# Attention core: the scores of a query tile move from two tiles ahead to three, with a third buffer of probabilities

## What is computed

```python
mask = key_chunk[None, :] <= q_chunk[:, None]
s = jnp.einsum('bqhd,bkhd->bhqk', q_blk, k).astype(jnp.float32) * scale
s = jnp.where(mask[None, None], s, neg)
prob = jax.nn.softmax(s, axis=-1).astype(v.dtype)
return jnp.einsum('bhqk,bkhe->bqhe', prob, v)
```

## Time and profile before

| | |
|---|---|
| median of 3 runs | 1248.72 us |
| profiled execution: its own time | 1248.54 us |
| its span, first to last instruction | 1246.7 us |
| granted TensorE clock, mean | 0.998 |
| TensorE busy (records of matmuls) | 1233.4 us, 99% |
| VectorE, ScalarE, GpSimd busy | 719.9, 483.8, 514.3 us |
| the four attention heads | from 281.6 to 391.1 us of the span |

### The profile page before, as it was taken

The page is one execution under the profiler, slowest core; times in us unless marked ns, Lnnn a source line. Parts: engine busy times, 40 slices in busy tenths (PEclk is TensorE's granted clock), DMA queues, the critical chain, the costliest instruction groups (busy, mean ns, idle before and its releaser), DMA issues.

```text
span 1246.7 us, 16762 instructions
## 1 busy us (share of the span) xinstructions
PE 1233.4 (99%) x6006; PEld 1040.8 (83%) x6006; DVE 719.9 (58%) x1172; ACT 483.8 (39%) x892; POOL 514.3 (41%) x515
## 2 busy tenths in 40 slices
PE   9999999999999999999999999999999999999997
PEld 8888888888898888888888888888888888888886
DVE  5544444466664437845444445444499999954433
ACT  7622222256664225533333333333354344424422
POOL 2533343351110003555533455433499889810011
PEclk9999999999999999999999999999999999999999
DMA  9511101000021500243332342422555545420002
GB/s 343 165 35 49 36 2 43 1 18 18 17 104 50 152 1 1 76 127 101 111 121 71 105 127 85 127 90 80 186 199 157 169 169 189 149 85 1 1 34 101
DMA packets 101931, 115.09 MB, mean 92 GB/s; under 512 B 4832, under 2 KB 67680, under 8 KB 101856
## 3 DMA queue, kind: packets, MB, share of 16 engines
q1 hardware_dynamic: 101424, 113.57, 28.0%
q10 hardware_dynamic: 432, 0.54, 0.1%
HBM read 90.49 MB, written 23.59 MB: 92 GB/s over the span
## 4 chain that ended last, share of the span: by engine, by line
PE 96%; DVE 2%; ACT 1%; issue 1%; DMA 0%; POOLq 0%; DVEq 0%; SPq 0%; POOL 0%; ACTq 0%
PE PS L1749 11%; PE PS L1750 11%; PE PS L1748 11%; PE PS L206 8%; PE PS L208 8%; PE PS L207 8%; PE PS L2082 5%; PE PS L2084 5%; PE PS L2083 5%; PE PS L1043 3%; PE PS L1059 3%; PE PS L2461 2%; PE PS L2460 2%; PE PS L2459 2%; PE PS L871 2%; PE PS L2474 2%
## 5 line engine op out<-in xcount | busy, mean ns | idle before, releaser
L206 PE MATMUL PS<-WF,HTH 128*128 128x512 f32 (+1 forms) x448 | 176.5, 394 | 0.2 <-DVE HTL L436 0.2
L208 PE MATMUL PS<-WF,HTL 128*128 128x512 f32 (+1 forms) x448 | 173.3, 387 | 0.0
L207 PE MATMUL PS<-WF,HTH 128*128 128x512 f32 (+1 forms) x448 | 172.9, 386 | 0.0
L1469 DVE TENSOR_TENSOR X<-X,PS 128x512 f32<-128x512 f32 x172 | 110.2, 678 | 54.4 <-PE PS L208 37.3
L1748 PE MATMUL PS<-HTH,WF 128*128 128x512 f32 x336 | 130.7, 389 | 0.0
L1749 PE MATMUL PS<-HTL,WF 128*128 128x512 f32 x336 | 130.7, 389 | 0.0
L1750 PE MATMUL PS<-HTH,WF 128*128 128x512 f32 x336 | 130.7, 389 | 0.0
L1681 DVE TENSOR_TENSOR WF<-RAW,WF 128x512 fp32r<-128x512 f32 x63 | 70.9, 1126 | 77.5 <-ACT WF L1671 77.5
L1748 PE MATMUL PS<-WF 128*128 128x512 f32 x252 | 98.0, 389 | 0.0
L1749 PE MATMUL PS<-WF 128*128 128x512 f32 x252 | 98.0, 389 | 0.0
L1750 PE MATMUL PS<-WF 128*128 128x512 f32 x252 | 98.0, 389 | 0.0
(11 more groups left out here) (266 smaller groups left out, 2808.0 us busy)
## 6 DMA issues: line engine op xcount, KB each, us to landing
hid<-TMP SPq DMA_DIRECT2D x74, 256.0 KB, 2.3
TMP<-hid SPq DMA_DIRECT2D x25, 512.0 KB, 4.4
RAW<-in_w_ffn_gate SPq DMA_DIRECT2D x22, 512.0 KB, 4.2
RAW<-in_w_ffn_up SPq DMA_DIRECT2D x22, 512.0 KB, 5.4
RAW<-in_w_ffn_down SPq DMA_DIRECT2D x22, 512.0 KB, 4.2
X<-in_x SPq DMA_DIRECT2D x16, 512.0 KB, 5.7
RAW<-in_w_in SPq DMA_DIRECT2D x32, 256.0 KB, 3.6
TAB<-hid SPq DMA_DIRECT2D x9, 512.0 KB, 4.6
```

The lines of the kernel that those rows point to most:

```text
L206: nc.tensor.matmul(dst, HTH[:, k, tok], w_h, start=(k == 0), stop=False)
L207: nc.tensor.matmul(dst, HTH[:, k, tok], w_l, start=False, stop=False)
L208: last = nc.tensor.matmul(dst, HTL[:, k, tok], w_h, start=False, stop=(k == K - 1))
L1469: nc.vector.tensor_tensor(x, x, src, ALU.add).then_inc(done, 1)
```

## The change

- TensorE: the filler is now `scores(t + 3)` in slots 0 to 4, and `early(0)`, `early(1)`, `early(2)` in slots 5, 6 and 7. Slot 1 is no longer without one.
- The next head's first queries (rows 0 to 511) are made in two halves of three matmuls (`first_queries`), one in slot 5 and one in slot 6; the second six matmuls (rows 512 to 1023) stay in slot 7. In head 3 the fillers of slots 5, 6 and 7 are two, one and one retention tiles.
- ScalarE: the exponentials go two tiles ahead: `exp(t + 2)` in slot t. The split of the next head's weights moves from slot 3 to slot 2, on VectorE too. The output weights' copies stay in slots 4 and 5.
- VectorE: slot t holds `divide(t + 1)`, `biggest(t + 3)`, `out_lo(t - 1)`.
- A third buffer of probabilities (JUNK, in TAB), and three columns each for biases and sums.
- The banks of scores are handed out in another order, and `scores(4)` waits for two exponentials instead of three.

The diff, cut to its core:

```diff
--- before.py
+++ after.py
@@ -977,6 +977,15 @@
             three(bank(2 + b), [([WQ[x][:, k] for x in range(2)], [CT[y][:, k, blk] for y in range(2)])
                                 for k in range(2)]).then_inc(a_proj, 1)
 
+        def first_queries(e, h, k):
+
+            if k == 0:
+                e.wait_ge(a_w_lo, h * 2 + 2)
+            for n, (x, y) in enumerate(((0, 0), (0, 1), (1, 0))):
+                last = nc.tensor.matmul(bank(2), WQ[x][:, k], CT[y][:, k, 0:HALF], start=(k + n == 0), stop=(k * n == 2))
+            if k == 1:
+                last.then_inc(a_proj, 1)
+
         def head_keys(e, h, blocks=(0, 1)):
 
             for b in blocks:
@@ -1017,7 +1026,12 @@
 
             return (1, (t + 1) * P) if t < 4 else (2, (t + 1) * P // 2)
 
-        SCORE_BANK = (2, 0, 3, 1, 2, 0, 2, 0)
+        SCORE_BANK = (2, 3, 0, 1, 2, 0, 2, 0)
+        BIAS, SUMS = 85, 88
+
+        def probs(t):
+
+            return JUNK if t % 3 == 2 else tmp((t % 3) * 1024, 1024)
 
         def score_banks(t):
 
@@ -1031,7 +1045,7 @@
                 if t in (0, 2):
                     e.wait_ge(a_qr, h * 2 + (2 if t else 1))
                 if t >= 4:
-                    e.wait_ge(a_exp, h * T + t - 1)
+                    e.wait_ge(a_exp, h * T + (2 if t == 4 else t - 1))
                 tok = slice(t * P, t * P + P)
                 nb, n = seen(t)
                 for c in range(nb):
@@ -1048,7 +1062,7 @@
                 e.wait_ge(a_pt, h * T + t)
                 for j in range(t + 1):
                     last = nc.tensor.transpose(PS[:, 4 + j // 4, (j % 4) * P:(j % 4) * P + P],
-                                               tmp((t % 2) * 1024 + j * P, P), ident)
+                                               probs(t)[:, j * P:j * P + P], ident)
                 last.then_inc(a_turn, 1)
 
             def values(t):
@@ -1062,14 +1076,11 @@
             for t in range(3):
                 scores(t)
             for t in range(T):
-                if t == 0:
-                    scores(3)
-                elif 2 <= t < T - 2:
-                    scores(t + 2)
-                elif t >= T - 2:
-
-                    e.wait_ge(a_exp, h * T + T - 1)
-                    early(t + 2 - T)
+                if t < T - 3:
+                    scores(t + 3)
+                else:
+                    e.wait_ge(a_exp, h * T + (T if t == T - 1 else T - 1))
+                    early(t + 3 - T)
                 if t >= 1:
                     values(t - 1)
                 turn(t)
@@ -1088,11 +1099,11 @@
         def act_head(e, h, early, late, after, turned=None):
             def exp(t):
                 e.wait_ge(a_bias, h * T + t + 1)
-                e.wait_ge(a_turn, h * T + max(0, t - 1))
+                e.wait_ge(a_turn, h * T + max(0, t - 2))
                 nb, n = seen(t)
-                dst = tmp((t % 2) * 1024, nb * n).rearrange("p (b n) -> p b n", b=nb)
-                nc.scalar.activation(dst, score_banks(t), ACT.Exp, bias=ST[:, 76 + t % 2:77 + t % 2],
-                                     scale=SCALE, accum_out=ST[:, 78 + t % 2:79 + t % 2]).then_inc(a_exp, 1)
+                dst = probs(t)[:, 0:nb * n].rearrange("p (b n) -> p b n", b=nb)
+                nc.scalar.activation(dst, score_banks(t), ACT.Exp, bias=ST[:, BIAS + t % 3:BIAS + 1 + t % 3],
+                                     scale=SCALE, accum_out=ST[:, SUMS + t % 3:SUMS + 1 + t % 3]).then_inc(a_exp, 1)
 
             def out_hi(t):
                 e.wait_ge(a_pv, h * T + t + 1)
@@ -1100,16 +1111,17 @@
                                bank(6 + t % 2, P).unsqueeze(1)).then_inc(a_o_hi, 1)
 
             exp(0)
+            exp(1)
             for t in range(T):
-                if t + 1 < T:
-                    exp(t + 1)
+                if t + 2 < T:
+                    exp(t + 2)
                 if turned and t == T - 1:
                     turned(1)
                 if t >= 1:
                     out_hi(t - 1)
                 if turned and t == T - 2:
                     turned(0)
-                if t == 3:
+                if t == 2:
                     early()
                 if t in (4, 5):
                     out_weights_hi(e, h, t - 4)
@@ -1126,7 +1138,7 @@
         def dve_head(e, h, early, after, turned=None):
             def biggest(t):
                 e.wait_ge(a_scores, h * T + t + 1)
-                e.wait_ge(a_exp, h * T + max(0, t - 1))
+                e.wait_ge(a_exp, h * T + max(0, t - 2))
                 src = score_banks(t)
                 nb, n = seen(t)
 
@@ -1135,7 +1147,7 @@
                 nc.vector.tensor_reduce(ST[:, 74 + t % 2:75 + t % 2], src, mybir.AxisListType.XY if nb > 1 else AXX,
                                         ALU.max).then_inc(a_max, 1)
                 e.wait_ge(a_max, h * T + t + 1)
-                nc.vector.tensor_scalar(ST[:, 76 + t % 2:77 + t % 2], ST[:, 74 + t % 2:75 + t % 2], -SCALE, None,
+                nc.vector.tensor_scalar(ST[:, BIAS + t % 3:BIAS + 1 + t % 3], ST[:, 74 + t % 2:75 + t % 2], -SCALE, None,
                                         ALU.mult).then_inc(a_bias, 1)
 
             def out_lo(t):
@@ -1147,26 +1159,27 @@
             def divide(t):
                 e.wait_ge(a_exp, h * T + t + 1)
                 n = (t + 1) * P
-                nc.vector.reciprocal(ST[:, 80 + t % 2:81 + t % 2], ST[:, 78 + t % 2:79 + t % 2]).then_inc(a_rec, 1)
+                nc.vector.reciprocal(ST[:, 80 + t % 2:81 + t % 2], ST[:, SUMS + t % 3:SUMS + 1 + t % 3]).then_inc(a_rec, 1)
                 e.wait_ge(a_rec, h * T + t + 1)
-                p = tmp((t % 2) * 1024, n)
+                p = probs(t)[:, 0:n]
                 nc.vector.tensor_scalar(p, p, ST[:, 80 + t % 2:81 + t % 2], None, ALU.mult).then_inc(a_prob, 1)
 
             biggest(0)
             biggest(1)
             divide(0)
+            biggest(2)
             for t in range(T):
-                if t + 2 < T:
-                    biggest(t + 2)
                 if t + 1 < T:
                     divide(t + 1)
+                if t + 3 < T:
+                    biggest(t + 3)
                 if turned and t == T - 1:
                     turned(1)
                 if t >= 1:
                     out_lo(t - 1)
                 if turned and t == T - 2:
                     turned(0)
-                if t == 3:
+                if t == 2:
                     early()
             after()
             out_lo(T - 1)
@@ -1178,17 +1191,23 @@
             e.wait_ge(b_qr, 5)
             head_keys(e, 0, [1])
 
+            def next_queries(b, h):
+                if b < 2:
+                    first_queries(e, h, b)
+                else:
+                    head_queries(e, h, 1)
+
             def next_keys(values, h):
                 head_keys(e, h)
                 values()
             with e.Fori(0, HEADS - 1) as h:
-                pe_head(e, h, lambda b: head_queries(e, h + 1, b), lambda values: next_keys(values, h + 1))
+                pe_head(e, h, lambda b: next_queries(b, h + 1), lambda values: next_keys(values, h + 1))
             e.wait_ge(r_done, NR)
 
             def first_turns(b):
                 if b:
                     e.wait_ge(a_exp, NR)
-                pe_retention_turn(e, (2 * b, 2 * b + 1))
+                pe_retention_turn(e, (b + 1,) if b else (0, 1))
 
             def out_products(values):
                 out_product(e, 0)
```

## The result

The changed kernel takes 1254.26 us (median of 6 runs, 1254.06 to 1254.96) where the kernel before takes 1249.01 (6 runs, 1248.57 to 1249.36): ratio 1.0045, 95% interval 1.0034 to 1.0055. It is slower by 5.2 us; forecast was 1253.5, range 1250.9 to 1255.4. The profiled execution took 1254.27 us with a span of 1252.4, against 1248.54 and 1246.7.

The account below looks back on a forecast made before the run. TensorE, busy 1233.4 of 1246.7 us, was taken as the bound. Heads 0 to 2 added 3.7 us and head 3 1.3, so 5.0 on 1248.54: 1253.5 us, range 1250.9 to 1255.4.

Parts of the forecast that it names:

- Slots 0 to 2: Front of heads 0 to 2: slot 1's gaps go, 1.02 us idle comes ahead of tile 5's scores; net +0.07 us each.
- Both old gaps: TensorE, slot 1: 0.64 us idle ahead of tile 0's values, 0.41 us ahead of tile 1's transposes; both would go.
- Slot 5, slot 6: Shorter fillers leave TensorE waiting for ScalarE's copy: 0.58 us idle ahead of tile 4's values, 0.55 us ahead of tile 5's.
- Heads 0 to 2: Each of the first three heads slower by 0.07 + 0.58 + 0.55 + 0.03 = 1.23 us, 3.7 in all.
- Head 3: Last head, retention transposes as fillers: 0.06 + 0.37 + 0.74 + 0.1 = 1.3 us slower.
- The rivals: Whole kernel: bubbles go, 1244.8 us (0.04); move is even, 1248.8 us (0.08); ScalarE gets behind, 1255.5 us and up (0.08).
- No buffer of probabilities was short: Slot 1's gaps: a skill rule blamed too few buffers, 3.7 us gain; the prediction said no buffer's release ends them.
- ScalarE did not fall behind: Third rival, slots 4 and 5: long exponentials of tiles 6 and 7 delay result and copy, 1255.5 us and up; chance 0.08.
- the second rival: The move is even: slots 1 and 2 only shift the gap, copies keep pace in slots 5 and 6; 1248.8 us, chance 0.08.
- the way without the weights: Slots 5 and 6, ScalarE's chain behind the values without the output weights' copy (0.52 us): 1.27 to 1.35 us.
- The unknowns that the prediction lists: Score start after a wait, -0.4 to +1.2 us over four heads; slots 5 and 6 waits, 0.2 each, 1.6 in all.
- its 3.7 us of idle time: TensorE's idle in slot 1 before the change: some 1.0 us each in heads 0, 1 and 2, 0.7 in head 3.

Follow-up runs that it names:

- The swap on VectorE: Changed kernel with the maximum of tile 3 ahead of the division of tile 1 on VectorE, nothing else: 1252.28 us.
- tile 7 split: Changed kernel with tile 7's scores cut in two over slots 4 and 5, its exponential in slot 6, queries whole in slots 6 and 7: 1250.06 us.
- split of tile 4 and two moves: Kernel before, changed banks, tile 4's scores halved over slots 1 and 2, output weights behind the copy, slot 7's copy between the query splits: 1245.38 us.

## Why the prediction was right

- *Slots 0 to 2.* Both old gaps went and one of 0.92 us came (1.02 forecast), at the place and with the releaser named; the hand-over was 0.06 and not 0.09, and values and transposes ahead of it ended 0.06 later in the head than laid out. Forecast +0.07; measured, from first score to first score of tile 6, 320.79 - 311.73 = 9.06 against 9.01 for the same work before (318.99 - 309.98): +0.05. The swap on VectorE shows the cause. The prediction said rightly that no buffer's release ends the old gaps. It named banks 0 and 1 for the new one, but did not draw from it that this gap is a wait for a buffer.
- *Slot 5, slot 6.* 0.58 and 0.55 forecast, 0.59 and 0.55 measured. Putting long fillers back (tile 7 split) takes them away.
- *Heads 0 to 2.* 1.23 forecast each, 1.36 measured. The term that was missing: behind a wait the values take longer, ten from 328.99 to 330.18 in 1.19 us where they took 1.12, twelve in 1.41 from 332.05 (to the transposes at 333.46) where they took 1.34. That is 0.07 us for each of the two new waits; why is not shown.
- *Head 3.* 1.3 forecast, 1.32 measured, and by the parts that were named. The scores of tile 6 start 379.93 - 371.26 = 8.67 us into the head, against 8.61 for the same work before: +0.06. The values of tile 4 start 388.00 - 386.32 = 1.68 us behind the end of those of tile 3 (1.67 forecast). From the end of the values of tile 4 to those of tile 5 it is 1.78 us, with four retention transposes between where there were eight and 1.79: as forecast, taking them out shortened nothing.
- *The rivals.* No buffer of probabilities was short (third buffer alone: 109.50 us against 109.49). Of the banks for the scores this is not shown: the kernel uses all eight, and no run gave tile 5 a bank that was free. ScalarE did not fall behind: in head 1 the exponential of tile 7 ended at 330.00, and ScalarE then waited 0.47 us for the values of tile 4. One sentence of the second rival was wrong: I put the way without the weights at 1.27 to 1.35 us. With them behind the copy, from the end of the values of tile 3 to the start of those of tile 4 it is 328.20 - 326.66 = 1.54 us, and 331.14 - 329.39 = 1.75 one tile later, since the copy waits for the transposes (0.19 us in its row). The same slip made the one large miss among the expectations.
- *The total.* 5.0 forecast, 5.40 in the heads, 5.25 between the medians of the two kernels.
- *What was off beside it.* The unknowns that the prediction lists add up to -2.0 and +2.8 us, which is 1251.5 to 1256.3; the range of 1250.9 to 1255.4 is not their sum. And its 3.7 us of idle time leave out a wait in heads 0 to 2 of the kernel before, 0.29 us ahead of the last values (334.86 to 336.62, less 1.47). It is in the changed kernel as well and moves no term of the forecast.

## What to carry to other kernels

A filler has to be counted over the whole loop: moving scores one slot ahead filled the empty slot at the front and took a filler from the end, where the wait for the copy had been hidden by it. Look at the length of what is moved: cutting a piece at its bank and spreading it over two slots gave 2.5 us, where moving it whole gave 0.5 us in the heads and nothing clear of the noise between the medians. And before giving a tile another buffer or an earlier place, ask whether its wait ends with a result or with the release of a buffer, of which buffer, and by what chain: here the old gaps ended with a copy and a division, the new one with a bank, and VectorE's work up to the fourth maximum set the earliest start for every order of TensorE that was tried.

## What was not expected of the hardware

- A copy out of PSUM on ScalarE starts 0.28 us after TensorE has gone on from the transposes to its next instruction (327.13 to 327.41), and values follow a copy by 0.10. The 0.28 stand elsewhere too, where the copy waits for the transposes (331.04 to 331.32 in head 1 of the kernel before). With the weights out of the way these 0.38 us were still there.
- A row of 128-column values matmuls takes 0.07 us longer to the transposes behind it when its first one had to wait (1.19 against 1.12 us for ten, 1.41 against 1.34 for twelve). With tile 7 split a wait of 0.10 us was enough for it (326.99 to 328.18, 1.19 for ten). The sixteen values at a head's end, which scores follow, do not show it: 1.78 us behind a wait of 0.29 (336.62 to 338.40, kernel before), 1.76 without one (334.84 to 336.60, split of tile 4 and two moves). Why is not shown.
